# Memory's values as the last projection chunk, head weights in the retention steps, and one unit for a head's three branches in tiles 0 and 1

## The chip, the core and the metric

The kernel runs on one core of a Trainium2 chip. A core has TensorE for matmuls (PE; PEld are its weight loads), VectorE (DVE), ScalarE (ACT), GpSimd (POOL) and SyncE (SP, which here issues most loads). They run their own streams and meet at semaphores. The metric is the time of one execution on the device in microseconds, lower is better.

## What is computed

One step of a hybrid decoder layer, for a prompt of 1024 tokens and a sample group of 8 sequences with 8 tokens each. One input projection feeds three groups of heads, and the mixed result goes through an output projection and a final norm:

```python
def mixer_inputs(x, ln_g, w_in):
    B, T = x.shape[:2]
    h = rmsnorm(x, ln_g) @ w_in
    q_n, kv_c, kv_s, kv_w, g_n, z_n, q_r, k_r, v_r, z_r, q_m, z_m = split_cols(h)
...
    o_n = nsa_prompt(q_n, kv_c, kv_s, kv_w, g_n, comp)
    o_r, st_r = retention_prompt(q_r, k_r, v_r, pos_p, ret_gn[l])
    mkv = mem_kv(mem_prompt, ln_mem[l], w_mem_kv[l])
    o_m = mem_attend(q_m, mkv)
    xp = finish(xp, o_n, z_n, o_r, z_r, o_m, z_m, w_out[l])
...
    o_n, new_win = nsa_sample(q_n, kv_c, kv_s, kv_w, g_n, comp, cache_nsa_cmp[l], cache_nsa_slc[l],
                              cache_nsa_win[l], page_table)
```

The NSA heads (8 query heads in 2 groups) attend in three branches, each with its own softmax: selected blocks (slc), a window of 512 keys (win), and compressed blocks (cmp); sigmoid gates mix them. With 1024 keys in blocks of 64 and 16 blocks selected, the prompt's selected branch is plain causal attention. The retention heads end in a norm for each head, `(o - mu) * rsqrt(var + EPS)`, times weights `g`. The memory heads attend to 256 memory tokens, whose keys and values are a projection too. The new K and V rows, the shifted window cache (`new_win_s`, 4 MB copied from input to output) and the states are outputs.

## The kernel before, in words

All matmuls of the projections work on float32 numbers split into a high and a low part, three products for each. The program has three stages.

**Trunk.** The projection is cut into 15 column chunks (`CHUNKS`; an entry is source, first column, width; source 1 is the memory's weights), each of 256 columns or a few more, and 9 row tiles (8 of prompt, one of the sample's 64 tokens; the memory's chunks have 2 tiles). That makes 121 jobs, run chunk by chunk; a job is 24 matmuls of 0.119 us. The job's result stands in one of four PSUM banks until ACT (`ACT_CHUNKS`) or DVE evicts it, with a silu where it is a gate; POOL stores it to DRAM. Each chunk's weights are loaded by SP and split by ACT (high part) and DVE (low part, L568). Between jobs stand small groups of steps for compression and retention. Retention takes one step for each row tile: `scores`, `norm`, `state` on DVE. `finish` (L1295) makes the norm's factors for all nine tiles at once and applies, for each tile, the factor (L1305) and the head weights `gnb` (L1306). SP's `load_k` (L668) waits for `r_done`, which these last operations raise, then loads K's rows (`pk_Ktok`) over memory that the retention used. PE's `ktr` steps (L918) transpose them, between the last jobs.

**Attention.** A table of blocks sets the order. A block is a row tile `i` and a group `g`; blocks of two tiles alternate, tile pairs (6,1), (7,0), (5,2), (4,3). A block has four units (l = 4g to 4g + 3), for heads g and g + 4: two are the selected branch of one head, two are the window and compressed branches of one head. The block of g = 4 has two memory units. There are 144 units, numbered v. In iteration v the loop places: scores `qk` (L1703, L1706, L1707) and row maxima `max` (L2031, DVE) of unit v + 2; the transposes of the probabilities of unit v (L1733), up to four key tiles a chunk, copied from PSUM by ACT or DVE in turn (L1900); the value matmuls `pv` (L1853) of a pair of units; the exponentials `sm` (L1963, ACT) of unit v + 2; and from v = 8 one group of the sample's steps. A group is a few steps: transposes of cached keys from SBUF (L1785), scores (L1717), probabilities transposed (L1810), values (L1821). The sample's caches come in four page pairs: SP loads the window pages (`s_WG`, L1598) and 16 selected pages (`s_SG`, L1601) of each pair.

Some steps hang on the number v alone:

```python
            if v == 36:
                steps.append(("copy_win", 0))
            if v % 4 == 0 and 36 < v <= 60:
                steps.append(("copy_kv", (v - 36) // 4 - 1))
```

`copy_win` (L1986) is one DMA on ACT's queue that copies the window cache from DRAM to DRAM; `copy_kv` (L1991) are smaller ones of new K and V rows.

**Output projection.** PE multiplies the mixed rows by the output weights, DVE adds and normalizes.

## Time and profile before

| | |
|---|---|
| runs | 950.6, 950.07, 946.06 us; median 950.07 |
| profiled execution | 949.89 us, span of the core 948.1 us |
| PE, DVE, ACT, POOL busy | 910.6, 513.5, 413.9, 289.5 us |
| DMA | 118.10 MB, mean 125 GB/s |

How to read it: times in the rows are microseconds from the span's start. In a timeline row stand start, duration, engine, line, operation, output<-input, shapes and count; in brackets at the end is the idle time of the engine before the row, with the instruction or DMA that ended it. Matmuls overlap, so the duration of one is longer than the distance to the next. A trailing q (SPq, ACTq) marks the engine's issuing of a DMA. "DMA to landing" is the time from issue to the DMA's end. The granted clock is 1.00 at 2.4 GHz and 0.50 at 1.2 GHz. The trunk ends at about 484 us.

### The profile page before, as it was taken

Reading aid. Unit: us, or ns where it says so; the run is one execution under the profiler, and the core shown is the slowest. Engines: PE = TensorE matmul, PEld = TensorE weight load, DVE = VectorE, ACT = ScalarE, POOL = GpSimd, SP = SyncE. Lnnn points to the kernel's source line nnn. Section 1 sums busy time; section 2 is a strip of 40 time slices with the busy share of each in tenths; the row PEclk is TensorE's granted clock in tenths of the full one; section 3 lists DMA queues with packets and bytes.
Section 4 is the critical chain, followed back from the end, with each engine's and each line's share of the span. In section 5 each row is a group of like instructions: output and inputs, shape, how many; then the busy total and the mean of one; then the engine's idle time right before and its main releaser. Section 6 shows DMA issues by size and latency. Waiting matters only on the chain.

```text
span 948.1 us, 20735 instructions
## 1 busy us (share of the span) xinstructions
PE 910.6 (96%) x7830; PEld 828.3 (87%) x7830; DVE 513.5 (54%) x1304; ACT 413.9 (44%) x1061; POOL 289.5 (31%) x495
## 2 busy tenths in 40 slices
PE   6999999999999999999889999999999999999997
PEld 6999999999999999999888788878877787878885
DVE  5556332323223556347536687766776757845443
ACT  7443221234344111222446666656665667832221
POOL 0213222212216353453144253334322525410000
PEclk9999999999999999999999999999999999999999
DMA  8554422404242543321868059714504142334331
GB/s 227 174 188 141 142 81 111 160 29 120 71 148 76 137 134 105 103 87 53 201 172 212 3 158 263 251 55 140 156 1 130 56 138 65 114 122 140 125 127 66
DMA packets 85076, 118.10 MB, mean 125 GB/s; under 512 B 12914, under 2 KB 67234, under 8 KB 84402
## 3 DMA queue, kind: packets, MB, share of 16 engines
q1 hardware_dynamic: 71522, 73.30, 27.0%
q0 software_dynamic: 10224, 36.20, 11.6%
q10 hardware_dynamic: 3232, 7.28, 2.1%
q8 instruction: 63, 1.03, 0.5%
q14 instruction: 35, 0.29, 0.1%
HBM read 91.68 MB, written 32.02 MB: 130 GB/s over the span
## 4 chain that ended last, share of the span: by engine, by line
PE 77%; DVE 6%; issue 5%; DMA 4%; ACT 3%; POOL 2%; SPq 2%; ACTq 0%; DVEq 0%; POOLq 0%
PE psum L1853 7%; PE psum L592 7%; PE psum L593 6%; PE psum L594 6%; PE psum L1733 5%; PE psum L1706 4%; PE psum L1872 3%; PE psum L1873 3%; PE psum L1874 3%; PE psum L1707 3%; PE psum L579 2%; PE psum L580 2%; PE psum L581 2%; PE psum L834 2%; PE psum L836 2%
## 5 line engine op out<-in xcount | busy, mean ns | idle before, releaser
L592 PE MATMUL psum<-a_whi,f_xhi 128*128 128x256 f32 (+1 forms) x672 | 195.2, 290 | 2.5 <-DVE f_xlo L1053 1.4
L593 PE MATMUL psum<-a_wlo,f_xhi 128*128 128x256 f32 (+1 forms) x672 | 190.9, 284 | 0.0
L594 PE MATMUL psum<-a_whi,f_xlo 128*128 128x256 f32 (+1 forms) x672 | 190.2, 283 | 0.0
L1963 ACT ACTIVATE p_P<-psum,p_nb 128x640 f32<-128x640 f32 (+7 forms) x224 | 124.1, 560 | 40.0 <-DVE p_nb L2031 37.9
L2031 DVE TENSOR_REDUCE p_nb<-psum 128x1 f32<-128x640 f32 (+7 forms) x224 | 110.2, 522 | 48.8 <-PE psum L1707 45.2
L592 PEld LDWEIGHTS psum<-a_whi,f_xhi 128*128 128x128 f32 x672 | 127.8, 190 | 5.2 <-DVE a_wlo L568 1.8
L593 PEld LDWEIGHTS psum<-a_wlo,f_xhi 128*128 128x128 f32 x672 | 127.8, 190 | 0.0
L594 PEld LDWEIGHTS psum<-a_whi,f_xlo 128*128 128x128 f32 x672 | 127.7, 190 | 0.0
L736 POOL DMA_DIRECT2D h_scratch<-a_hst x93 | 51.1, 552 | 228.8 <-DVE a_hst L1114 105.6
L1733 PE MATMUL psum<-f_ident,p_P 128*128 128x128 f32 x656 | 99.7, 276 | 1.1 <-ACT s_KTw L1912 0.5
L1733 PEld LDWEIGHTS psum<-f_ident,p_P 128*128 128x128 f32 x656 | 77.7, 141 | 7.2 <-DVE p_PT L1900 1.7
L568 DVE SCALAR_TENSOR_TENSOR a_wlo<-a_wraw,c_gcol,a_whi 128x256 fp32r<-128x256 f32 (+1 forms) x120 | 55.4, 524 | 43.0 <-ACT a_whi L555 42.9
L1900 ACT COPY p_PT<-psum 128x512 f32<-128x512 f32 (+3 forms) x107 | 56.3, 526 | 47.6 <-PE psum L1733 46.6
L1123 DVE TENSOR_TENSOR c_ctlo<-psum,c_cthi 128x512 fp32r<-128x512 f32 (+1 forms) x40 | 25.4, 636 | 93.7 <-ACT c_cthi L1008 93.7
L1853 PE MATMUL psum<-p_PT,p_V 128*64 128x128 f32 x1056 | 71.8, 279 | 1.7 <-issue 1.3
L1008 ACT CAST c_cthi<-psum 128x512 fp32r<-128x512 f32 (+1 forms) x40 | 21.8, 544 | 106.3 <-PE psum L817 106.3
L1853 PEld LDWEIGHTS psum<-p_PT,p_V 128*64 128x64 f32 x1056 | 56.4, 136 | 12.4 <-issue 10.8
L2210 POOL TENSOR_TENSOR p_Oi<-p_Oi 128x128 f32<-128x128 f32 x32 | 16.6, 518 | 129.9 <-DVE p_Oi L2053 129.9
L579 PE MATMUL psum<-f_xhi,a_whi 128*128 128x256 f32 x192 | 55.6, 290 | 0.0
L1900 DVE COPY p_PT<-psum 128x512 f32<-128x512 f32 (+3 forms) x109 | 54.4, 499 | 1.2 <-PE psum L1733 1.2
L580 PE MATMUL psum<-f_xhi,a_wlo 128*128 128x256 f32 x192 | 54.1, 282 | 0.0
L581 PE MATMUL psum<-f_xlo,a_whi 128*128 128x256 f32 x192 | 53.8, 280 | 0.0
(334 smaller groups left out, 2139.2 us busy)
## 6 DMA issues: line engine op xcount, KB each, us to landing
a_wraw<-in_w_in SPq DMA_DIRECT2D x24, 512.0 KB, 4.4
h_scratch<-a_hst POOLq DMA_DIRECT2D x72, 128.0 KB, 3.5
s_SG<-in_cache_nsa_slc SPq DMA_DIRECT2D x64, 128.0 KB, 2.2
p_qd<-q_scratch SPq DMA_DIRECT2D x16, 384.0 KB, 7.7
a_xraw<-in_x_prompt SPq DMA_DIRECT2D x8, 512.0 KB, 6.8
s_MK<-in_cache_mem SPq DMA_DIRECT2D x8, 512.0 KB, 9.3
s_WG<-in_cache_nsa_win SPq DMA_DIRECT2D x8, 512.0 KB, 4.6
mix_scratch<-p_zt POOLq DMA_DIRECT2D x8, 512.0 KB, 3.4
```

The source lines that it names most:

```text
L568: ins = nc.vector.scalar_tensor_tensor(out=lo[:, k], in0=raw[:, k], scalar=split_gain(e, 4 * half + k), in1=hi[:, k].bitcast(F32), op0=ALU ...
L579: nc.tensor.matmul(out, wh, hi, start=first, stop=False)
L580: nc.tensor.matmul(out, wl, hi, start=False, stop=False)
L581: return nc.tensor.matmul(out, wh, lo, start=False, stop=last)
L592: nc.tensor.matmul(out, hi, wh, start=first, stop=False)
L593: nc.tensor.matmul(out, hi, wl, start=False, stop=False)
L594: return nc.tensor.matmul(out, lo, wh, start=False, stop=last)
L1733: l = nc.tensor.transpose(o[0:w, 128 * j:128 * j + 128], P[v % 2][:, at:at + w], ident[:])
L1853: i_mm = nc.tensor.matmul(psum[64 * j:64 * j + 64, at:at + 128], val, PTs[p_rank[pair[j]] % NPT][0:w, 128 * p:128 * p + 128], start=k == 0 ...
L1900: copy(PTs[r % NPT][0:w, 0:128 * n], bank(4 + c % 3)[0:w, 0:128 * n]).then_inc(sem, 1)
L1963: nc.scalar.activation(dst, s_view(s), ACT.Exp, bias=nb[:, g % NNB:g % NNB + 1], accum_out=ssum[:, par[i], s[1]:s[1] + 1]).then_inc(S("p_e ...
L2031: nc.vector.tensor_reduce(out=nb[:, g % NNB:g % NNB + 1], in_=s_view(s), op=ALU.max, axis=AX.X if len(s[6]) == 1 else AX.XY, negate=True). ...
```

## The change

1. The memory's value chunk moves from place 8 to the last place of the projection. ACT evicts it, with a scaled copy. The other chunks, their weights and splits come earlier by its two jobs. Its load for the attention (`VM`) moves from `load_k` to the start of the sample's loads and is waited for at the first memory unit.
2. The multiplication with `gnb` moves from `finish` into `norm` of each retention step, and `load_k` waits for those only. The last operations of `finish` follow later; `ktr` waits for the last state too.
3. ACT's load of the exponential's table, and DVE's low parts of the first Q tile (`qlo`), stand before the last two evictions of the trunk. Before, the table load was the attention's first step.
4. In tiles 0 and 1 (`WHOLE`) a unit (l >= 18) is all three branches of one head, so such a block has 2 units where it had 4, and there are 128 units. Two groups of the sample's steps are placed in such an iteration, except for the eight groups that begin with the first page pair's load. The copies out of `OT` (the values' transposes) are written before each new one. The numbers 36 and 40 to 60 in the code above stay.

```diff
--- before.py
+++ after.py
...
 CHUNKS = [(0, 512, 256), (0, 768, 256), (0, 1816, 256), (0, 2072, 256), (0, 2328, 256), (0, 1024, 280), (1, 0, 256), (0, 1304, 256),
-          (1, 256, 256), (0, 256, 256), (0, 2840, 256), (0, 0, 256), (0, 1560, 256), (0, 2584, 256), (0, 3096, 256)]
+          (0, 256, 256), (0, 2840, 256), (0, 0, 256), (0, 1560, 256), (0, 2584, 256), (0, 3096, 256), (1, 256, 256)]
 NCH = len(CHUNKS)
...
     BLOCKS = [(pair[j], g) for pair in PAIRS for j, g in ((0, 0), (0, 1), (1, 0), (1, 1), (0, 2), (1, 2), (1, 3), (1, 4), (0, 3), (0, 4))]
-    UNITS = [(i, l) for i, g in BLOCKS for l in (range(4 * g, 4 * g + 4) if g < 4 else (16, 17))]
+    WHOLE = (0, 1)
+    UNITS = [(i, l) for i, g in BLOCKS for l in ((16, 17) if g == 4 else (18 + 2 * g, 19 + 2 * g) if i in WHOLE else range(4 * g, 4 * g + 4))]
     NV = len(UNITS)
-    unit_block = [b for b, (i, g) in enumerate(BLOCKS) for _ in range(4 if g < 4 else 2)]
+    unit_block = [b for b, (i, g) in enumerate(BLOCKS) for _ in range(2 if g == 4 or i in WHOLE else 4)]
     last_of_block = {b: v for v, b in enumerate(unit_block)}
...
     assert all(prev[i] is None or of_tile[prev[i]][-1] < of_tile[i][0] for i in range(QT))
-    per_unit = lambda l: 1 if l < 16 and l % 4 < 2 else 2
+    per_unit = lambda l: 3 if l >= 18 else 1 if l < 16 and l % 4 < 2 else 2
     sm_before = [sum(per_unit(l) for _, l in UNITS[:v]) for v in range(NV)]
...
-    ACT_CHUNKS = (5, 7, 12, 13, 14)
-    MEM_CHUNKS = (6, 8)
-    Q_CHUNKS = (11, 9, 10)
+    ACT_CHUNKS = (5, 7, 11, 12, 13, 14)
+    MEM_CHUNKS = (6, 14)
+    Q_CHUNKS = (10, 8, 9)
...
                     steps.append(("load_w", fill.pop(0)[1]))
+        steps.extend([("table", 0), ("qlo", 0), ("qlo", 1), ("qlo", 2)])
         evict(0)
...
                 sp.wait_ge(S("r_stout"), 16 * 6)
-                wait_stored(sp, last_job[11])
+                wait_stored(sp, last_job[10])
                 for br, c in enumerate((C_KVS, C_KVW)):
...
                     sp.dma_start(V[:, br], hD[0:T, c + 128:c + 256].rearrange("(t p) n -> p t n", p=128)).then_inc(S("p_v"), 16)
-                sp.dma_start(VM[:], new_mem[:, 256:512].rearrange("(t p) n -> p t n", p=128)).then_inc(S("p_v"), 16)
...
                 pe.wait_ge(S(f"p_k{n // 2}"), 16)
+                pe.wait_ge(S("r_ns"), 4)
                 pe.wait_ge(S("r_done"), NT)
...
                 split_hi(act, n, (int(what == "split_b"),))
+            elif what == "table":
+                act.wait_ge(S("r_done"), 2 * NT)
+                nc.scalar.activation(small[:, 152:153], ident[:, 0:1], ACT.Exp).then_inc(S("p_table"), 1)
             elif what == "ev" and by_act(proj_jobs[n][0]):
...
                 act.wait_ge(S("x_rs"), NT + 2)
-                if j == 5:
+                if j == NCH - 1:
+                    nc.scalar.activation(dst[:, 0:256], src, ACT.Copy, scale=rstd(t)).then_inc(S("h_evac_act"), 1)
+                elif j == 5:
                     nc.scalar.activation(dst[:, 0:256], src[:, 0:256], ACT.Copy, scale=rstd(t)).then_inc(S("h_part"), 1)
...
                     nc.vector.tensor_tensor(lv, src, hv.bitcast(F32), ALU.subtract).then_inc(S("p_klo"), 1)
-            elif what == "qtr":
+            elif what == "qlo":
                 dve.wait_ge(S("q0_hi"), n + 1)
...
             ch.step(nc.vector.tensor_tensor(rsq[0:r], OC[0:r, n], OC[0:r, n], ALU.mult))
-            ch.step(nc.vector.tensor_reduce(out=var, in_=rsq[0:r].rearrange("p (h e) -> p h e", h=4), op=ALU.add, axis=AX.X))
+            ch.do(nc.vector.tensor_reduce(out=var, in_=rsq[0:r].rearrange("p (h e) -> p h e", h=4), op=ALU.add, axis=AX.X))
+            nc.vector.tensor_tensor(OC[0:r, n], OC[0:r, n], gnb[0:r], ALU.mult).then_inc(S("r_done"), 1)
+            ch.wait()
...
                 oc = OC[0:r, n].rearrange("p (h e) -> p h e", h=4)
-                ch.step(nc.vector.tensor_tensor(oc, oc, rs[0:r, 4 * n:4 * n + 4].rearrange("p (h o) -> p h o", o=1).to_broadcast([r, 4, HD]), ALU.mult))
-                nc.vector.tensor_tensor(OC[0:r, n], OC[0:r, n], gnb[0:r], ALU.mult).then_inc(S("r_done"), 1)
+                dve.wait_ge(S("r_done"), NT)
+                nc.vector.tensor_tensor(oc, oc, rs[0:r, 4 * n:4 * n + 4].rearrange("p (h o) -> p h o", o=1).to_broadcast([r, 4, HD]), ALU.mult).then_inc(S("r_done"), 1)
...
         base, at = 1024 * ((v + 1) % 2), sm_before[v]
+        if l >= 18:
+            g, j = (l - 18) // 2, l % 2
+            h, n = g + 4 * j, 128 * (i + 1)
+            return [(at, 6 * g + j, 0, h, 0, n, [(base, n)], 0), (at + 1, 6 * g + 2 + j, 1, h, 0, n, [(base + 512 + NC, n)], 256),
+                    (at + 2, 6 * g + 4 + j, 2, h, 0, 64, [(base + 512, NC)], 640)]
         if l >= 16:
...
         i, l = UNITS[v]
+        if l >= 18:
+            h, n = softmaxes(v)[0][3], softmaxes(v)[0][5]
+            base = softmaxes(v)[0][6][0][0]
+            return [(base, n, KS[:, h // 4, 0:n], h), (base + 512, NC + n, KW[:, h // 4, 0:NC + n], h)]
         if l < 16 and l % 4 >= 2:
...
             n = unit_block[v]
-            if v == last_of_block[n] and a == 1 and 128 * (k + 1) >= softmaxes(v)[a][5]:
+            if v == last_of_block[n] and a == len(softmaxes(v)) - 1 and 128 * (k + 1) >= softmaxes(v)[a][5]:
+                while outs:
+                    write(outs.pop(0)[0])
                 steps.append(("ot", n))
...
         groups = sample_groups()
+        n_groups = len(groups)
+        paged = next(k for k, g in enumerate(groups) if ("load_pair", 0) in g)
         first = 8
...
                 mine.append(add_p(v, tiles[f:f + 4]))
-                if l >= 16:
+                if l in (16, 17):
                     waiting.append((mine[-1], mine[-1]))
...
             partner = mine
-            while waiting and (l % 2 == 0 or l >= 16) and waiting[0][1] not in mine:
+            while waiting and (l % 2 == 0 or l == 17) and waiting[0][1] not in mine:
                 pv()
...
                     steps.append(("load_q", later[k]))
-            for what, n in groups.pop(0) if v >= first and groups else []:
-                if what == "t":
-                    add(n)
-                else:
-                    steps.append((what, n))
+            for _ in range(2 if l >= 18 and not 0 <= n_groups - len(groups) - paged < 8 else 1):
+                for what, n in groups.pop(0) if v >= first and groups else []:
+                    if what == "t":
+                        add(n)
+                    else:
+                        steps.append((what, n))
             if v == 36:
...
         load_mem(1)
+        sp.dma_start(VM[:], new_mem[:, 256:512].rearrange("(t p) n -> p t n", p=128)).then_inc(S("p_k2"), 16)
         for o, c, w in ((0, C_ZN, 512), (512, C_ZR, 256), (768, C_ZM, 256)):
...
+        first_mem = min(v for v in range(NV) if any(s[2] == 3 for s in softmaxes(v)))
+
         def pv(pair):
...
             if pair[0] == p_index[0]:
-                pe.wait_ge(S("p_v"), 48)
+                pe.wait_ge(S("p_v"), 32)
+            if v == first_mem:
+                pe.wait_ge(S("p_k2"), 32)
             wait_chunks_read(pe, pair)
-            if l >= 16:
+            if l in (16, 17):
                 sides = [[(p, k, 128) for p, (a, k, _) in enumerate(p_chunks[pair[0]][2]) if a == j] for j in range(2)]
...
                     p, k, w = sides[j][m]
-                    vj = v if l >= 16 else v + j
-                    a = j if l >= 16 else p_chunks[pair[j]][2][p][0]
+                    vj = v if l in (16, 17) else v + j
+                    a = j if l in (16, 17) else p_chunks[pair[j]][2][p][0]
                     _, num, b, h, k0, keys = softmaxes(vj)[a][0:6]
...
     def act_attend(act):
-        nc.scalar.activation(small[:, 152:153], ident[:, 0:1], ACT.Exp).then_inc(S("p_table"), 1)
         act.wait_ge(S("h_mm"), len(proj_jobs))
...
```

DVE at the end of the trunk. Before, the tail of the norm, with `f_OC` the retention outputs and `r_gnb` the head weights:

```order
L1298 TENSOR_SCALAR f_small<-f_small 128x36
L1300 RECIPROCAL f_small<-f_small 128x36
L1310 TENSOR_TENSOR f_small<-f_small 128x36
L1311 TENSOR_TENSOR f_small<-f_small 128x36
L1312 TENSOR_SCALAR f_small<-f_small 128x36
L1313 TENSOR_TENSOR f_small<-f_small 128x36
L1305 TENSOR_TENSOR f_OC<-f_OC,f_small 128x256
L1306 TENSOR_TENSOR f_OC<-f_OC,r_gnb 128x256
```

After, in the same place, behind the last state (`r_kvt`, `r_BDs`):

```order
L1298 TENSOR_TENSOR r_kvt<-r_kvt,r_BDs 128x512
L1300 TENSOR_SCALAR r_BDs<-r_kvt,f_colc 128x2x128 x2
L1307 TENSOR_SCALAR f_small<-f_small 128x36
L1309 RECIPROCAL f_small<-f_small 128x36
L1319 TENSOR_TENSOR f_small<-f_small 128x36
L1320 TENSOR_TENSOR f_small<-f_small 128x36
L1321 TENSOR_SCALAR f_small<-f_small 128x36
L1322 TENSOR_TENSOR f_small<-f_small 128x36
L1315 TENSOR_TENSOR f_OC<-f_OC,f_small 128x256 x8
L1315 TENSOR_TENSOR f_OC<-f_OC,f_small 64x256
```

The multiplications with `r_gnb` have left the tail; one stands in each retention step.

ACT where trunk and attention meet. `a_hst` are evicted rows, `p_P` the probabilities of the first units. Before:

```order
L996 ACTIVATE a_hst_70<-psum,f_small 128x256
L996 ACTIVATE a_hst_71<-psum,f_small 128x256
L996 ACTIVATE a_hst_68<-a_hst_68,f_small 64x256
L1940 ACT_TABLE_LOAD
L1940 ACTIVATE f_small<-f_ident 128x1
L1963 ACTIVATE p_P_119,p_ssum<-psum,p_nb 128x896
L1963 ACTIVATE p_P_120,p_ssum<-psum,p_nb 128x896
```

After:

```order
L1003 ACTIVATE a_hst_69<-psum,f_small 128x256
L1003 ACTIVATE a_hst_70<-a_hst_70,f_small 64x256
L985 ACT_TABLE_LOAD
L985 ACTIVATE f_small<-f_ident 128x1
L998 ACTIVATE a_hst_71<-psum,f_small 128x256
L998 ACTIVATE a_hst_68<-psum,f_small 128x256
L1990 ACTIVATE p_P_119,p_ssum<-psum,p_nb 128x896
L1990 ACTIVATE p_P_120,p_ssum<-psum,p_nb 128x896
```

The table load has moved ahead of the last two evictions, and these are now the memory's values.

ACT around the copy of the window cache. Before, `s_KTs` are the sample's transposed selected keys, and 128x1024, 128x640 the exponentials of tile 7's first units:

```order
L1963 ACTIVATE p_P_119,p_ssum<-psum,p_nb 128x640
L1963 ACTIVATE p_P_119,p_ssum<-psum,p_nb 128x64
L1912 COPY s_KTs<-psum 128x512
L1986 DMA out_new_win_s<-in_cache_nsa_win 8x8x16128
L1900 COPY p_PT_147<-psum 128x512
L1963 ACTIVATE p_P_120,p_ssum<-psum,p_nb 128x640
L1963 ACTIVATE p_P_120,p_ssum<-psum,p_nb 128x64
L1946 ACTIVATE s_PW,s_ssm<-s_PW,s_snb 128x576
L1900 COPY p_PT_129<-psum 128x512
L1963 ACTIVATE p_P_119,p_ssum<-psum,p_nb 128x1024
```

After, 128x128 and 128x64 are those of tile 0's whole units and 128x1088 the sample's selected keys of a sequence pair:

```order
L1990 ACTIVATE p_P_119,p_ssum<-psum,p_nb 128x128 x2
L1990 ACTIVATE p_P_119,p_ssum<-psum,p_nb 128x64
L1973 ACTIVATE s_PSl,s_ssm<-s_PSl,s_snb 128x1088
L2013 DMA out_new_win_s<-in_cache_nsa_win 8x8x16128
L1928 COPY p_PT_145<-psum 128x384
L1990 ACTIVATE p_P_120,p_ssum<-psum,p_nb 128x128 x2
L1990 ACTIVATE p_P_120,p_ssum<-psum,p_nb 128x64
L1946 COPY s_PTS<-psum 128x512
L2011 COPY p_OT<-psum 128x384
L1990 ACTIVATE p_P_119,p_ssum<-psum,p_nb 128x1024
```

The copy's issue has moved from the first unit of block (7,0) to the first of block (0,0), behind an exponential of the sample.

## Rows read from the trace of the kernel before

**Rows 1.** Page, busy time: engine, us, share of the span, instructions.

```profile
PE 910.6 (96%) x7830; PEld 828.3 (87%) x7830; DVE 513.5 (54%) x1304; ACT 413.9 (44%) x1061; POOL 289.5 (31%) x495
```

**Rows 2.** Waits of PE, whole span: line, releaser; us in total, times, longest.

```profile
PE psum L1703 <- ACT p_P L1963: 4.2, 6, 1.4
```

**Rows 3.** Timeline 442 to 461 us: start, us, engine, line, op, out<-in, count [idle before].

```profile
442.68 3.26 DVE L568 SCALAR_TENSOR_TENSOR a_wlo<-a_wraw,c_gcol,a_whi 128x256 fp32r<-128x256 f32 x8
...
447.66 0.42 DVE L1305 TENSOR_TENSOR f_OC<-f_OC,f_small 128x256 f32<-128x256 f32 x1
...
454.47 0.42 DVE L1306 TENSOR_TENSOR f_OC<-f_OC,r_gnb 64x256 f32<-64x256 f32 x1
...
454.91 1.01 SPq L668 DMA_DIRECT2D pk_Ktok<-h_scratch  x2
...
460.25 1.41 PE L918 MATMUL psum<-f_ident,pk_Ktok 128*128 128x128 f32 x8 [3.71 <-DMA pk_Ktok<-h_scratch]
```

**Rows 4.** Lines L661 and L668: ns min/median/max, first and last start; time to landing.

```profile
L661 SPq DMA_DIRECT2D out_new_ret_s<-r_BDs x4: 596/642/649, 442.7 to 444.7; - x4
...
DMA to landing us min/median/max: 2.6/2.7/2.7
...
L668 SPq DMA_DIRECT2D pk_Ktok<-h_scratch x2: 386/482/577, 454.9 to 455.3; - x2
...
DMA to landing us min/median/max: 5.3/6.0/6.7
```

**Rows 5.** Windows: stretch, length, busy us of each engine, PE clock, DMA share, GB/s.

```profile
460.30:464.20 3.90, 3.90 (x21) 3.90 (x22) 2.55 (x4) 2.79 (x5) 0.60 (x3) 0.57 1.14 286
488.00:492.00 4.00, 3.94 (x22) 3.88 (x23) 1.42 (x3) 2.05 (x5) 4.00 (x8) 0.57 0.66 174
...
597.90:604.00 6.10, 6.10 (x89) 5.64 (x87) 2.74 (x9) 3.25 (x16) 4.20 (x8) 1.00 1.05 322
```

**Rows 6.** Timeline 485 to 489 us, ACT and then PE.

```profile
485.00 0.51 ACT L996 ACTIVATE a_hst<-a_hst,f_small 64x256 f32<-64x256 f32 x1 [3.25 <-DVE a_hst L1099]
485.52 1.28 ACT L1940 ACT_TABLE_LOAD   x1
486.82 0.20 ACT L1940 ACTIVATE f_small<-f_ident 128x1 f32<-128x1 f32 x1
...
485.56 0.23 PE L1703 MATMUL psum<-p_maskb,f_identb 128*128 128x128 bf16 x1 [1.51 <-ACT a_hst L996]
...
488.06 0.37 PE L1703 MATMUL psum<-p_maskb,f_identb 128*128 128x128 bf16 x3 [1.40 <-ACT p_P L1963]
```

**Rows 7.** Timeline 584 to 587 us, PE.

```profile
584.59 1.31 PE L1853 MATMUL psum<-p_PT,p_V 128*64 128x128 f32 x20
585.73 0.39 PE L1853 MATMUL psum<-p_PT,f_VC 128*64 128x128 f32 x4
586.05 0.66 PE L1785 MATMUL psum<-f_ident,s_SG 128*128 128x128 f32 x4
```

**Rows 8.** Timeline, ACT's DMA issues of units 36 and 44.

```profile
573.89 0.83 ACTq L1986 DMA_DIRECT2D out_new_win_s<-in_cache_nsa_win  x1
...
596.02 0.51 ACTq L1991 DMA_DIRECT2D out_new_slc_p<-h_scratch  x1
```

**Rows 9.** DMA queues, 575.5 to 597.9 us: queue; packets, MB, share of 16 engines.

```profile
q10 hardware_dynamic: 640, 4.58, 52.9%
```

**Rows 10.** Tile p_qd, 577 to 579 us: issues, and time to landing.

```profile
L692 SPq DMA_DIRECT2D p_qd<-q_scratch x2: 573/614/655, 577.1 to 577.7; - x2
...
DMA to landing us min/median/max: 7.3/17.9/28.4
```

**Rows 11.** Timeline 606 to 626 us, SP and then PE.

```profile
606.27 17.27 SPq L1601 DMA_DIRECT2D s_SG<-in_cache_nsa_slc  x16
...
618.60 0.60 PE L1785 MATMUL psum<-f_ident,s_WG 128*128 128x128 f32 x4
...
625.51 0.63 PE L1785 MATMUL psum<-f_ident,s_SG 128*128 128x128 f32 x4 [0.47 <-DMA s_SG<-in_cache_nsa_slc]
```


## The prediction, made before the change was timed

> **What bounds the kernel now.** I read the engines' busy time first: PE works 910.6 of 948.1 us [rows 1], so a change pays only where it takes idle time, low clock or work from PE, and it costs where it makes PE wait. The waits of PE by cause come next: six on the exponentials before score matmuls sum to 4.2 us [rows 2], and three waits at the end of the trunk, each seen beside its row in the timeline, are among the largest of all. Then I followed those backwards: who released PE, and what held that one.
>
> The sum is made against the profiled execution, 949.89 us. The median of the three runs is 950.07, so no correction is needed between them.
>
> **Part 1: the head weights and memory's last chunk.** At the end of the trunk DVE splits a weight chunk in eight operations from 442.68 us (3.26 us), then runs the GroupNorm's tail: from 447.66 us nine pairs of dependent operations, the last one starting at 454.47 [rows 3]. SP has waited for that and issues the load of K's rows at 454.91; the first of its two loads lands 5.3 us later [rows 3, 4]. PE has finished its matmuls at 456.5, stands for 3.71 us and starts the K transposes at 460.25 [rows 3].
> The change moves nine multiplications by the head weights into the retention steps (0.42 us each, beside matmuls, where DVE is busy 54% of the time [rows 1]) and takes the K load out from behind the tail. What releases the load then is the last state store. Those four stores were issued over 2.0 us from 442.7 and each takes 2.7 us to land [rows 4]. In the new order half of a weight split (some 1.6 of the 3.26 us) stands ahead of the last state, so the stores end at about 442.7 + 1.6 + 2.1 + 2.7 = 449.1, and the first K load lands at 449.1 + 5.3 = 454.4, ahead of PE's 456.5. PE's new wait there, for the states, ends well before it arrives; behind it stand the K transposes and all the rest of PE. The wait goes. So does what follows it: from 460.3 to 464.2 the granted clock is 0.57 [rows 5], that is between 1.2 GHz (0.50) and 2.4 GHz, after 3.71 us without work. Low clock costs 3.90 x (1 - 0.57) = 1.7 us. **Part 1: -5.4 us**, between -6.0 and 0 (zero if the load is still late by another path; the memory K load behind it has the same slack).
> Moving the memory value chunk to the end reorders the same 121 jobs. Every job finds its weights split two jobs sooner or later; the matmuls are the same in number. The memory values are loaded after the sample's cache reads, and are first used by a pair of memory units tens of us later: nothing.
>
> **Part 2: the switch from trunk to attention.** After the last projection matmuls PE waits 1.51 us at 485.56 for ACT's silu of the last sample job (485.00, 0.51 us, after two DVE additions), and 1.40 us at 488.06 for the exponential of unit 0, which stands behind the 1.28 us load of the exponential's table at 485.52 and a first tiny activation at 486.82 [rows 6]. Afterwards, 488 to 492, the clock is 0.57 [rows 5]: 4.0 x 0.43 = 1.7 us. In all 1.51 + 1.40 + 1.7 = 4.6 us. The last chunk's silu is now a plain scaled copy without the DVE additions, and the table load stands two evictions earlier, hidden by matmuls. ACT waits there for the GroupNorm's tail, with two evictions queued behind it; the tail, now nine operations, is over by some 453 us, nearly 30 us sooner. What is late next is the maximum of unit 1 and its exponential: 0.3 to 0.7 us remain before the third unit's scores, and part of the low clock. I take **-3.4 us**, between -4.6 (nothing left) and -1.3 (only the table hidden).
> Of the table: the load takes 1.28 us and the next activation starts 1.30 us after it, so hiding it is worth 1.3 us by the row. The Trainium skill (ScalarE: Activation LUTs, What ACT_TABLE_LOAD costs) gives 1283 ns for the load, which the trace agrees with, plus about 1380 ns of drain, which no gap in these rows shows; by the page the switch would be worth 2.66 us, and the sum some 1.3 us lower.
>
> **Part 3: three branches in one unit, tiles 0 and 1.** 32 units of two kinds become 16; the matmuls are the same. PE gains where sequences merge: four value matmuls at 585.73 take until 586.05, 0.32 us, while twenty before them took 1.14 us, 0.057 each [rows 7], so the end of a group costs 0.32 - 0.23 = 0.09 us, and its start about as much by the same way of reading: 0.2 us a group. Eight groups fewer give 1.5 us. ACT's and DVE's copies of transposed probabilities become fewer and larger. Idle PE time in these tiles' blocks is short, part of the 4.2 us of [rows 2]. But a longer chain (three maxima, then three exponentials) stands between a unit's scores and its transposes, with two sample groups popped per unit, so that dependent sample steps come closer to each other. I take **-2.3 us**, between -5 (all idle gone too) and +5 (each of eight joints exposed by 0.6 us, a little under the 0.7 us, 4.2/6, that a wait of rows 2 lasts at the mean).
>
> **Part 4: what the renumbering moves.** The copy of the window cache (4 MB, issued by ACT) hangs on unit number 36. Before, unit 36 is the first of block (7,0) and the copy is issued at 573.89; another copy, of unit 44, the first of block (0,0), is issued at 596.02 [rows 8]. After, tile 1's blocks have 8 units fewer, so unit 36 is the first of (0,0): **the big copy is issued where 596 to 598.6 is now**, about 24 us later. What does it do while it runs? From 575.5 to 597.9 its queue takes 52.9% of the time of all 16 DMA engines [rows 9]. Of the two loads of the next tile's Q issued at 577.1 and 577.7 one needs 7.3 us to land and the other 28.4 [rows 10]. So a load beside the copy in effect lands only after it ends: its packets alternate with far larger ones.
> Before, that stretch lies between the loads of the sample's first page pair and those of the second, whose 16 page loads are issued from 606.27 on, over 17.27 us; PE turns the window pages from 618.60 and the first selected page at 625.51, where it waits 0.47 us for the DMA already [rows 11]. After, the second pair's loads start some ten us behind the copy's issue and beside it. The copy starts 1.6 us after its issue and runs 22.4, so it ends between 620 and 622.6; I take the later, as it stands behind an exponential in its unit. Then 3 MB are waiting (1 MB window, 2 MB selected pages), half of them on the engines that the copy held. At the 322 GB/s of 597.9 to 604 [rows 5] that takes 9.8 us, at the pace of the K load (1 MB in 7.1 us from 454.91, less 2 us of start: 5 us a MB [rows 4]) 15 us. Window pages would be there at 626 to 628. PE has more prompt work before their second transposes in the new order, my estimate is 4.2 us, so that in the old frame it wants them at 618.6 + 4.2 = 622.8: 3.2 to 5.3 us of wait. The selected pages follow until 632.4 to 637.6, against a want of 625.9 plus that wait: 3 to 6 us more, so 8 to 11.5 us together, and low clock after each long wait as in parts 1 and 2, 1.7 us or a little more. **+12.3 us**, from 0 (the loads get through) to +17.
> The Trainium skill (DMA: Bandwidth & Descriptors, Queues, rings and completion order) states that each DMA engine goes round robin between its queues packet by packet. By that rule a queue of small packets beside one of large packets gets few bytes; with rows 9 and 10 the trace agrees.
>
> **Sum.** 949.89 - 5.4 - 3.4 - 2.3 + 12.3 = 951.1; forecast **951 us**, within 0.5%. A measurement here tells about 0.5% from no change: 4.75 us, 945.3 to 954.8.
>
> **Rivals.**
> *The page loads get through* (chance 0.29). For: half of the first Q load's bytes moved early, the copy holds only half of the engines, and pages are small. Against: 28.4 us in rows 10. Then parts 1 to 3 stand alone: 949.9 - 11.1 = 938.8; with a collision of a third of the size 943.
> *The collision is large and the whole units cost* (0.20). Mechanism: at the second page pair PE waits for pages at 15 us for 3 MB, and because two sample groups are popped per unit it meets page after page with nothing between; with part 3 at +2: 949.9 - 5.4 - 3.4 + 2 + 14 = 957. It decides from a collision above 13 us, or part 3 above +2 with 12.
> *The trunk's end doesn't do what it says* (0.05). K's load could stay late, since the transposes now wait for the states as well. Without part 1, and with the collision: 956.5. For: the state stores are a chain of their own. Against: 2.1 us of slack worked out above.
> *As forecast, gains cancelled* (0.46), own range 945.5 to 954.5.
>
> **How the numbers follow.** Faster by over 0.5%: 0.29. Within: 0.46. Slower: 0.20 + 0.05 = 0.25. The range takes in the first rival from its clean value of 938.8 and the second to 958.
>
> **What would show it.** Part 1: no idle PE before the K transposes and clock 1.00 behind them. Part 2: table load before the last two evictions, PE waits of under 1 us before the second and third unit's scores. Part 3: fewer and larger copies, 1 to 2 us less PE time in tiles 1 and 0. Part 4: the large copy issued at about 585 to 590 us of the new span (11 earlier by parts 1 to 3), Q and page loads landing in over 10 us, PE waits with page transposes as the waiting line, 5 us or more, and a clock of 0.5 to 0.6 behind them. The forecast is wrong if those page transposes don't wait, or if a wait comes up in the first tiles that no row of before shows.

## The result: slower by 1.2%

| | runs | median us | ratio to before (95%) |
|---|---|---|---|
| before | 4 | 948.58 | |
| after | 4 | 960.21 (959.09 to 961.93) | 1.0121 (1.0103 to 1.0139) |

The profiled execution of after has a span of 960.1 us, against 948.1. The forecast was 951, the range ended at 958: wrong, and on the side of slower.

### The profile page after: what moved, and what is told of

It is laid out like the page before. It is cut to its first block, busy times and chain, and to the rows that moved or that the text cites. A ratio compares the mean times of both kernels' runs of the same rounds, so it can differ in the third digit from the quotient of the medians.

```text
span 960.1 us, 20679 instructions
## 1 busy us (share of the span) xinstructions
PE 915.8 (95%) x7830; PEld 831.3 (87%) x7830; DVE 516.9 (54%) x1298; ACT 414.4 (43%) x1059; POOL 289.0 (30%) x495
## 3 DMA queue, kind: packets, MB, share of 16 engines
q8 instruction: 63, 1.03, 0.4%
## 4 chain that ended last, share of the span: by engine, by line
PE 78%; DVE 6%; issue 5%; ACT 4%; DMA 2%; SPq 2%; POOL 2%; ACTq 0%; DVEq 0%; POOLq 0%
PE psum L1881 8%; PE psum L594 7%; PE psum L595 7%; PE psum L596 7%; PE psum L1757 5%; PE psum L1730 3%; PE psum L1900 3%; PE psum L1901 3%; PE psum L1902 3%; PE psum L1731 3%; PE psum L835 2%; ACT p_P L1990 2%; PE psum L837 2%; PE psum L836 2%; PE psum L581 2%
## 5 line engine op out<-in xcount | busy, mean ns | idle before, releaser
L2058 DVE TENSOR_REDUCE p_nb<-psum 128x1 f32<-128x640 f32 (+8 forms) x224 | 109.3, 523 | 54.3 <-PE psum L1731 47.4
L1990 ACT ACTIVATE p_P<-psum,p_nb 128x640 f32<-128x640 f32 (+8 forms) x224 | 123.8, 561 | 29.8 <-DVE p_nb L2058 27.3
L1757 PE MATMUL psum<-f_ident,p_P 128*128 128x128 f32 x656 | 97.6, 276 | 4.0 <-ACT s_PTS L1946 1.7
L570 DVE SCALAR_TENSOR_TENSOR a_wlo<-a_wraw,c_gcol,a_whi 128x256 fp32r<-128x256 f32 (+1 forms) x120 | 63.7, 592 | 27.0 <-ACT a_whi L557 26.8
L2237 POOL TENSOR_TENSOR p_Oi<-p_Oi 128x128 f32<-128x128 f32 x32 | 14.5, 454 | 154.0 <-DVE p_Oi L2080 154.0
L1928 DVE COPY p_PT<-psum 128x512 f32<-128x512 f32 (+3 forms) x104 | 52.0, 500 | 1.3 <-PE psum L1757 1.1
```

The lines of the kernel that those rows point to most:

```text
L570: ins = nc.vector.scalar_tensor_tensor(out=lo[:, k], in0=raw[:, k], scalar=split_gain(e, 4 * half + k), in1=hi[:, k].bitcast(F32), op0=ALU ...
L1757: l = nc.tensor.transpose(o[0:w, 128 * j:128 * j + 128], P[v % 2][:, at:at + w], ident[:])
L1928: copy(PTs[r % NPT][0:w, 0:128 * n], bank(4 + c % 3)[0:w, 0:128 * n]).then_inc(sem, 1)
L1990: nc.scalar.activation(dst, s_view(s), ACT.Exp, bias=nb[:, g % NNB:g % NNB + 1], accum_out=ssum[:, par[i], s[1]:s[1] + 1]).then_inc(S("p_e ...
L2058: nc.vector.tensor_reduce(out=nb[:, g % NNB:g % NNB + 1], in_=s_view(s), op=ALU.max, axis=AX.X if len(s[6]) == 1 else AX.XY, negate=True). ...
```

## The profile after

PE's busy time, in the page's row of the engines, answers to [rows 1]:

```profile
PE 915.8 (95%) x7830; PEld 831.3 (87%) x7830; DVE 516.9 (54%) x1298; ACT 414.4 (43%) x1059; POOL 289.0 (30%) x495
```

5.2 us more busy, for the same 7830 matmuls, and the mean granted clock of the core fell from 0.995 to 0.985. The other part is waiting. PE's waits in the whole span, the largest that are new, against [rows 2] (in a row: who waited, for what; us in total, times, longest; "issue" means that the profile shows no one that PE waited for):

```profile
PE psum L1809 <- DMA s_SG<-in_cache_nsa_slc: 3.6, 1, 3.6
PE psum L1741 <- ACT s_KTs L1940: 2.9, 2, 2.4
PE psum L1809 <- DMA s_WG<-in_cache_nsa_win: 2.5, 1, 2.5
...
PE psum L1842 <- issue: 2.3, 2, 1.8
PE psum L581 <- DVE a_hst L1119: 2.0, 2, 1.8
```

Four of the five lie in the sample's steps: pages (`s_SG`, `s_WG`), the copy of their transposes (`s_KTs`), and value matmuls (L1842). The last, for DVE's eviction of a projection job (`a_hst`), stands in the trunk.

The end of the trunk, DVE, SP and PE, in the timeline, answers to [rows 3]:

```profile
450.16 3.10 DVE L1315 TENSOR_TENSOR f_OC<-f_OC,f_small 128x256 f32<-128x256 f32 x9
...
453.22 1.00 SPq L670 DMA_DIRECT2D pk_Ktok<-h_scratch  x2
...
460.46 1.04 PE L920 MATMUL psum<-f_ident,pk_Ktok 128*128 128x128 f32 x8
```

The tail of the norm is six and more products without a wait between them (2.10 us for six); the K load is issued at 453.22, and PE's transposes start at 460.46 with no idle time ahead of them. The missing wait came as forecast, though the issue is four us later than the forecast's 449.1; PE gets there four us later too. The switch to attention, which answers to [rows 6], came in part: waits of 0.57 and 1.18 us where 1.51 and 1.40 stood (both were to be under 1), and the clock behind them is 1.00 instead of 0.57 (the last row is a window, with the columns of [rows 5]).

```profile
483.22 0.23 PE L1727 MATMUL psum<-p_maskb,f_identb 128*128 128x128 bf16 x1 [0.57 <-ACT a_hst L998]
...
485.49 0.32 PE L1727 MATMUL psum<-p_maskb,f_identb 128*128 128x128 bf16 x3 [1.18 <-ACT p_P L1990]
...
485.00:490.00 5.00, 4.51 (x38) 4.40 (x39) 3.28 (x7) 4.37 (x11) 4.27 (x9) 1.00 0.59 153
```

Then the second page pair. In the timeline, ACT's issue of the big copy, SP's issues of window and selected pages, and PE's transposes and scores of them; this answers to [rows 8] and [rows 11]:

```profile
592.96 0.84 ACTq L2013 DMA_DIRECT2D out_new_win_s<-in_cache_nsa_win  x1
...
604.79 0.96 SPq L1621 DMA_DIRECT2D s_WG<-in_cache_nsa_win  x2
606.54 22.21 SPq L1624 DMA_DIRECT2D s_SG<-in_cache_nsa_slc  x16
...
621.97 1.94 PE L1809 MATMUL psum<-f_ident,s_WG 128*128 128x128 f32 x8 [2.52 <-DMA s_WG<-in_cache_nsa_win]
...
631.35 1.09 PE L1809 MATMUL psum<-f_ident,s_SG 128*128 128x128 f32 x4 [3.55 <-DMA s_SG<-in_cache_nsa_slc]
...
638.74 1.98 PE L1741 MATMUL psum<-s_KTs,s_QP 128*64 128x512 f32 x4 [2.43 <-ACT s_KTs L1940]
```

The copy goes out at 592.96, almost twelve us ahead of the window pages. The sixteen page issues take 22.21 us instead of 17.27. PE waits 2.52, 3.55 and 2.43 us. The times to landing of the window pages and of the sixteen selected ones, one line each, median in the middle:

```profile
DMA to landing us min/median/max: 5.9/11.2/16.6
...
DMA to landing us min/median/max: 2.2/4.3/11.2
```

A window load needs up to 16.6 us, a page up to 11.2; before it was 6.9 and 4.5 in the same places. The clock through the waits, with the columns of [rows 5]:

```profile
620.00:624.00 4.00, 2.03 (x12) 2.00 (x12) 0.81 (x3) 1.03 (x7) 0.00 (x0) 0.70 0.86 263
624.00:628.00 4.00, 3.80 (x15) 1.77 (x12) 1.50 (x6) 1.79 (x8) 0.00 (x0) 0.50 0.85 256
628.00:632.00 4.00, 0.65 (x3) 0.68 (x4) 0.91 (x2) 0.42 (x1) 0.00 (x0) 0.50 0.68 225
632.00:636.00 4.00, 4.00 (x28) 3.36 (x27) 1.31 (x4) 0.62 (x2) 0.00 (x0) 0.59 0.01 4
```

PE runs at 0.50 to 0.70 for sixteen us. So the loads are late beside the copy, where it was forecast. The question for the runs was how large it is, and what else costs.

## The experiments

Twelve kernels ran, each beside the kernel before, whose median was 949.2 us with e1 to e4, 948.93 with e5 to e8 and 948.85 with e9 to e12. The last column is the ratio's distance from 1, times 949 us. Differences of the medians give up to 1.2 us more or less (2.9 for e10), so a tenth of a us means nothing here.

| run | median us | ratio (95%) | that is, of 949 us |
|---|---|---|---|
| e1: after, copies where they were | 954.42 | 1.0050 (1.0030 to 1.0070) | +4.7 |
| e2: before, copies moved | 962.58 | 1.0143 (1.0094 to 1.0192) | +13.6 |
| e3: after, no whole units | 944.96 | 0.9963 (0.9942 to 0.9984) | -3.5 |
| e4: after, copy in small pieces | 959.25 | 1.0110 (1.0064 to 1.0156) | +10.4 |
| e5: e3, split of chunk 9 earlier | 943.19 | 0.9948 (0.9931 to 0.9964) | -4.9 |
| e6: before, head weights alone | 945.00 | 0.9963 (0.9949 to 0.9977) | -3.5 |
| e7: whole units in tile 1 alone | 948.94 | 1.0007 (0.9991 to 1.0024) | +0.7 |
| e8: e1, one group a unit in tile 0 | 948.45 | 0.9997 (0.9977 to 1.0018) | -0.3 |
| e9: e2, copy in small pieces | 954.58 | 1.0054 (1.0036 to 1.0072) | +5.1 |
| e10: before, small copies moved | 951.76 | 1.0018 (0.9999 to 1.0036) | +1.7 |
| e11: e1, the two groups apart | 947.07 | 0.9975 (0.9962 to 0.9989) | -2.4 |
| e12: tile 1, groups apart, split earlier | 945.51 | 0.9956 (0.9937 to 0.9975) | -4.2 |

### Copies back in their place (e1)

```diff
-            if v == 36:
+            if v == 28:
                 steps.append(("copy_win", 0))
-            if v % 4 == 0 and 36 < v <= 60:
-                steps.append(("copy_kv", (v - 36) // 4 - 1))
+            if v in (32, 36, 38, 40, 44, 46):
+                steps.append(("copy_kv", (32, 36, 38, 40, 44, 46).index(v)))
```

> The changed kernel, with the big window-cache copy and the six small copies back at the blocks where the kernel before has them: the big one at unit 28, the first of block (7,0), the small ones at units 32, 36, 38, 40, 44, 46. Nothing else differs. Theory A (the copy beside the second page pair's loads costs the time): the waits of PE on window and selected pages vanish, the stretch from block (7,2) to (7,3) gets back 14 to 17 us, and the time is 943 to 947 us. Theory B (the whole units and the doubled sample groups cost it, the copy is only there): the time stays within 3 us of the changed kernel's 960, and the waits move to scores and probabilities in tile 0's blocks.

954.4 us: neither. 1.0121 - 1.0050 is 6.7 us given back by the copies (the two intervals allow 4 to 9), but 8.3 us remain against e3, which has no whole units. PE's waits:

```profile
PE psum L1809 <- DMA s_SG<-in_cache_nsa_slc: 2.9, 1, 2.9
PE psum L1741 <- ACT s_KTs L1940: 2.5, 2, 2.0
PE psum L1842 <- issue: 2.3, 2, 1.8
```

The wait for the window pages is gone. The wait for a selected page (2.9), for the copy of transposes (2.5) and at L1842 (2.3) are still there, with no copy of the window cache beside them. The pages themselves land in 2.0 to 3.7 us, as before; PE asks for them sooner. So a second cause exists, and these waits lie in and beside tile 0's blocks. What the wait for `s_KTs` is made of, in order of time, ACT and PE:

```profile
630.96 1.06 PE L1809 MATMUL psum<-f_ident,s_SG 128*128 128x128 f32 x4
...
632.54 0.78 ACT L1973 ACTIVATE s_PW<-s_PW,s_snb 128x576 f32<-128x576 f32 x1
...
633.30 0.59 ACT L1940 COPY s_KTs<-psum 128x512 f32<-128x512 f32 x1
...
634.03 1.08 PE L1741 MATMUL psum<-s_KTs,s_QP 128*64 128x512 f32 x4 [2.01 <-ACT s_KTs L1940]
```

PE has transposed pages and stands until ACT has copied the result. ACT takes the copy in its turn, behind two exponentials of a memory unit and one of the sample (L1973). The 1.8 us at L1842 are of the same kind: there the copy of the transposed probabilities, 601.16 to 601.75, stands behind an exponential of 128x1024, and PE starts at 601.85.

### The copies alone, moved in the kernel before (e2, e10)

e2 is the kernel before with

```diff
-            if v == 36:
+            if v == 44:
                 steps.append(("copy_win", 0))
-            if v % 4 == 0 and 36 < v <= 60:
-                steps.append(("copy_kv", (v - 36) // 4 - 1))
+            if v in (52, 56, 64, 68, 72, 76):
+                steps.append(("copy_kv", (52, 56, 64, 68, 72, 76).index(v)))
```

and e10 has the second half of it only (the big copy stays at unit 36).

> The kernel before, with only the copies moved: the big one from unit 36 to unit 44, the first of block (0,0), the small ones from units 40 to 60 to units 52, 56, 64, 68, 72, 76, which are the blocks where the changed kernel has them. Theory A: 10 to 15 us slower than before, 959 to 964 us, with PE waiting for window and selected pages and a low clock behind each wait. Theory B: no difference, within 2 us of 949.

> The kernel before with the big copy at its place (unit 36) and only the six small copies moved to units 52 to 76. If the small copies take their part in the 13.4 us, 951 to 955 us, with PE waiting for selected pages; if the big copy alone does it, 948 to 950 us.

e2: 13.6 us slower (8.9 to 18.2). PE's two waits, in the timeline; then the window loads' and the sixteen page issues' rows (the duration of an issue in ns, min/median/max, and the window loads' time to landing):

```profile
624.01 1.09 PE L1785 MATMUL psum<-f_ident,s_WG 128*128 128x128 f32 x4 [6.41 <-DMA s_WG<-in_cache_nsa_win]
...
635.73 1.09 PE L1785 MATMUL psum<-f_ident,s_SG 128*128 128x128 f32 x4 [3.09 <-DMA s_SG<-in_cache_nsa_slc]
...
DMA to landing us min/median/max: 6.0/12.9/19.7
...
L1601 SPq DMA_DIRECT2D s_SG<-in_cache_nsa_slc x16: 337/338/9114, 605.4 to 631.1; - x16
```

6.41 and 3.09 us of waiting, with low clock behind each (0.50 over 624 to 628 us, 0.66 over 635 to 640). A window load took up to 19.7 us. One page issue kept SP for 9114 ns instead of 338, and SP handed out no load in that time. e10 shows the part of the small copies, 1.7 us (an interval that just touches none): their issues lie beside the page loads, and PE waits 3.21 us for a page instead of 0.47.

```profile
626.40 0.63 PE L1785 MATMUL psum<-f_ident,s_SG 128*128 128x128 f32 x4 [3.21 <-DMA s_SG<-in_cache_nsa_slc]
...
619.92 0.51 ACTq L1991 DMA_DIRECT2D out_new_slc_p<-h_scratch  x1
```

### Pieces of 4 KB instead of 64 KB (e4, e9)

```diff
-                act.dma_start(io["new_win_s"][0, :, 0:WIN - DS].rearrange("b t a k d -> b (t a k d)").rearrange("b (c e) -> b c e", c=16),
...
+                for d in range(2):
+                    act.dma_start(io["new_win_s"][0, :, 0:WIN - DS].rearrange("b t a k d -> b (t a k d)").rearrange("b (c f e) -> b f c e", c=63, f=2)[:, d],
...
```

> The changed kernel, copy at unit 36 as it is, but cut into pieces of 4 KB instead of 64 KB: two DMAs of 8 x 63 pieces, every second piece each, the same bytes. Theory A1 (the loads are starved because engines alternate between queues piece by piece, and the copy's pieces are large): page loads land in 3 to 6 us beside the copy, PE's waits for pages shrink below 2 us together, the time is 944 to 949 us. Theory A2 (the copy takes bytes, whatever their pieces): the page loads still land after the copy ends and the time stays at 957 to 962 us.

> The kernel before with the copies moved as in the run with the big copy at unit 44 (962.6 us), and the big copy cut into pieces of 4 KB. If the pieces' size starves the page loads, most of the 13.4 us come back: 950 to 954 us. If the bytes do, or the small copies that follow, 959 to 963 us.

On the kernel before (e9) it gives back 8.4 of the 13.6 us (3.5 to 13.4 by the two intervals); one wait for the sample's loads is left:

```profile
621.17 1.09 PE L1785 MATMUL psum<-f_ident,s_WG 128*128 128x128 f32 x4 [3.93 <-DMA s_WG<-in_cache_nsa_win]
...
DMA to landing us min/median/max: 6.3/11.8/17.2
```

The window load's worst time falls only from 19.7 to 17.2 us, but the wait for a selected page is gone. On the changed kernel (e4) almost nothing comes back: 1.0 us, within an interval of 4.7 us to either side. There the wait moved, from the window pages to a selected page:

```profile
PE psum L1809 <- DMA s_SG<-in_cache_nsa_slc: 7.2, 1, 7.2
...
DMA to landing us min/median/max: 3.7/5.6/9.9
```

The median page load takes 5.6 us there against 4.3 in after. So piece size matters on the kernel before, and it isn't all there: the copy's bytes and the small copies stay beside the loads, and no run parts the two. Why the same edit is worth 8.4 us on one kernel and 1 on the other was not settled; the changed kernel asks for its pages sooner, which is the next finding.

### No whole units (e3), and in tile 1 alone (e7)

```diff
-    WHOLE = (0, 1)
+    WHOLE = ()
```

> The changed kernel with no tile in WHOLE: four units a block everywhere, 144 units, so the copies stand where they stand before; memory's values last, head weights in the retention steps, table load early remain. Both theories of the collision: none here. By the block starts of the two traces the trunk's parts are worth 2.2 us at the first maximum and 4.2 us four units later: 944.5 to 947 us. If moving the copy (the run with the copy at unit 28) and this one give the same time, whole units are worth nothing.

> The changed kernel with whole units in tile 1 alone (tile 0 has four units a block again), the copies at the blocks of the kernel before (the big one at unit 28, the first of block (7,0)). By the block starts of the two traces whole units in tile 1 gain 0.8 us and in tile 0 with its doubled sample groups lose 8. Theory C (tile 0 loses): 943.5 to 946 us. If whole units lose in both tiles, 949 or more.

e3 came as expected: the trunk's parts are worth 3.5 us together. e7 didn't: it is 4.2 us slower than e3, so whole units with two groups in tile 1 lose too. Two of PE's waits, at block (2,2), where e3 has one of 0.24 us:

```profile
701.94 0.66 PE L1757 MATMUL psum<-f_ident,p_P 128*128 128x128 f32 x4 [1.03 <-ACT p_PT L1928]
...
703.50 0.44 PE L1757 MATMUL psum<-f_ident,p_P 128*128 128x128 f32 x2 [0.57 <-ACT s_PTS L1946]
```

The sample's steps have moved against the blocks. These two waits can hardly be what makes e7 slow, though: e11 and e12 below have them as well (1.03 and 0.58 us in e12), at 947.07 and 945.51 us. e7's runs spread from 947.3 to 953.4 us, the longer ones at a lower mean clock (0.994 against 0.999), and the profiled one is among the shortest. Where the 4.2 us lie stays open.

### Two groups together (e8, e11)

Both have the copies where e1 has them. e8 places one sample group in an iteration of tile 0 (`l >= 18 and i == 1` for two), and two in each of the later iterations 92 to 95. e11 keeps two and sets them apart:

```diff
             partner = mine
+            if l >= 18 and not 0 <= n_groups - len(groups) - paged < 8:
+                place_group()
             while waiting and (l % 2 == 0 or l == 17) and waiting[0][1] not in mine:
...
-            for _ in range(2 if l >= 18 and not 0 <= n_groups - len(groups) - paged < 8 else 1):
...
+            place_group()
```

> The changed kernel with whole units in both tiles and the copies at the blocks of the kernel before, but one sample group an iteration in tile 0 instead of two; four later iterations (92 to 95) take two so that all groups find a place. Theory C (the selected pages come one in 1.08 us, and the doubled groups ask for them sooner): the 2.9 us wait for a page and the 2.0 us wait for its copy go, 944 to 948 us. Theory D (the whole units' own chain of three maxima and exponentials costs it): the loss in tile 0's blocks stays, 951 to 955 us.

> The changed kernel with the copies at the blocks of the kernel before (as in the run with the copy at unit 28), and the two sample groups of a whole unit's iteration apart: one right behind the transposes of the unit, before its value matmuls, the other at the iteration's end as before. The pace of the groups and the whole units stay. Theory C2 (two groups standing together are the cost: the second one asks for pages a unit sooner, and meets copies that the first has just asked for): 945 to 950 us against 954.4. Theory D (whole units' own chains): 953 to 956 us.

e11 gives back 7.1 of the 8.3 us with whole units and all their softmaxes unchanged. PE's waits in it, the largest behind the one for `in_ln_mem`:

```profile
PE psum L1813 <- DMA s_SG<-in_cache_nsa_slc: 2.8, 1, 2.8
PE psum L1731 <- ACT p_P L1994: 2.1, 4, 1.2
```

The page wait stands (2.8), but the wait of 2.0 us for `s_KTs` and that of 1.8 us at L1842 are gone from the list (L1846 here). Low clock is part of the loss too. The stretch 620 to 650 us in e1, e11 and e3, with the columns of [rows 5]:

```profile
620.00:650.00 30.00, 24.94 (x168) 19.24 (x166) 17.31 (x37) 14.64 (x42) 7.36 (x13) 0.83 0.11 31
...
620.00:650.00 30.00, 27.57 (x231) 22.41 (x233) 19.57 (x40) 16.78 (x45) 12.85 (x19) 0.89 0.21 51
...
620.00:650.00 30.00, 28.16 (x270) 23.02 (x271) 21.50 (x49) 20.05 (x59) 14.01 (x22) 1.00 0.20 48
```

That is 5.1, 3.3 and 0 us of low clock. All of PE's waits from 484 to 945 us sum to 21.3, 15.7 and 14.0 us in the three traces. From e1 to e11 that makes 5.6 us of waiting and 1.8 of clock, near the measured 7.1. In e8, where the second group of each unit comes later by a unit or more, the page wait goes too, and with it the low clock (1.00 over 620 to 650):

```profile
PE psum L1727 <- ACT p_P L1990: 3.2, 7, 1.2
```

So the units' own chain of three maxima and exponentials is at most a small part of the cost: e11 is 1.1 us over e3. Two groups side by side are most of it. What a step leaves to ACT is wanted by the next step at once, while the copy stands behind ACT's exponentials; with value matmuls between the groups PE has work in that time. The page wait has another reason, the pace of two groups a unit: the pages are wanted sooner, from loads that SP issues one by one in 17.3 us. e11 keeps that pace and the wait, e8 loses both. e8 is still 3.2 us over e3, and its runs spread from 944.9 to 952.4 us; that rest was not taken apart.

### The trunk: head weights alone (e6), and a split beside GpSimd (e5)

e6 is the kernel before with only the edits in `norm` and `finish` and the wait for `r_ns`. e5 is e3 with the split of weight chunk 9 moved:

```diff
-                if j + 1 < NCH and i == (0 if j in MEM_CHUNKS else 4):
+                if j + 1 < NCH and i == (0 if j in MEM_CHUNKS else 1 if j == 8 else 4):
...
-                if j + 1 < NCH and i == (1 if j in MEM_CHUNKS else 5):
+                if j + 1 < NCH and i == (1 if j in MEM_CHUNKS else 2 if j == 8 else 5):
```

> The kernel before, with one part of the change alone: the multiplication by the head weights in each retention step, K's load released by those, the last state waited for before the K transposes. Chunk order, table load and units as before. Predicted share of the trunk: the 2.4 to 3.7 us wait before the K transposes is gone and the low clock behind it, where there was one: 944 to 946.5 us. If the gain of the trunk came from the table load and the last chunk instead, 948 to 949.

> The changed kernel with no whole units, and with the split of weight chunk 9 three jobs earlier, at jobs 1 and 2 of chunk 8 instead of 4 and 5, so that it runs on DVE before GpSimd's first two rope steps. Theory R (the split is slow because GpSimd's tensor operations run beside it: one operation took 3.19 and 3.42 us instead of 0.47): no split operation over 1.2 us there, the 1.8 us wait of PE near 306 us is gone, 942 to 943.5 us against 945 without the move. Theory S (the split is slow for its own sake or its data): the long operations move with it, and the time stays at 945 within 1 us.

e6 alone gives the 3.5 us that the three edits of the trunk give together in e3. That points to a cost in the others that eats their gain. One shows in the timeline of after, at the first retention steps, DVE, then POOL, then PE, and last the line's own row:

```profile
297.44 8.29 DVE L570 SCALAR_TENSOR_TENSOR a_wlo<-a_wraw,c_gcol,a_whi 128x256 fp32r<-128x256 f32 x4
...
297.51 2.81 POOL L783 TENSOR_TENSOR r_rtmp<-r_rr,r_rt 128x256 f32<-128x256 f32 x4
...
302.65 2.78 POOL L783 TENSOR_TENSOR r_rtmp<-r_rr,r_rt 128x256 f32<-128x256 f32 x4
...
306.12 0.38 PE L581 MATMUL psum<-f_xhi,a_whi 128*128 128x256 f32 x1 [1.83 <-DVE a_hst L1119]
...
L570 DVE SCALAR_TENSOR_TENSOR a_wlo<-a_wraw,c_gcol,a_whi x120: 466/481/3425, 7.4 to 470.4; 128x256 fp32r<-128x256 f32 x112, 128x280 fp32r<-128x280 f32 x8
```

Four split operations take 8.29 us on DVE; of the 120 in the trace the median is 481 ns, and the largest 3425 (the last row, ns min/median/max). GpSimd runs its rope steps at that time, and DVE's eviction, behind the split, keeps PE 1.83 us. In e5 the same eight operations stand before the rope:

```profile
287.86 1.68 DVE L570 SCALAR_TENSOR_TENSOR a_wlo<-a_wraw,c_gcol,a_whi 128x256 fp32r<-128x256 f32 x4 [6.41 <-ACT a_whi L557]
...
291.58 1.65 DVE L570 SCALAR_TENSOR_TENSOR a_wlo<-a_wraw,c_gcol,a_whi 128x256 fp32r<-128x256 f32 x4
...
297.42 2.82 POOL L783 TENSOR_TENSOR r_rtmp<-r_rr,r_rt 128x256 f32<-128x256 f32 x4
```

1.68 and 1.65 us, the wait near 306 is gone, and the time is 943.19 us. The step from e3 to e5 is 1.4 us by the ratios, whose intervals overlap, so the gain in time is likely and not shown; that the split is slow beside its neighbour the rows show, in both orders. The Trainium skill (SBUF — State Buffer, SBUF: two separate sides) says that VectorE operations with two SBUF inputs and GpSimd operations that read SBUF take a shared pair of ports as an exclusive lock for a whole instruction. The split reads two SBUF tensors. Two of its operations took 3.19 and 3.42 us, each over four GpSimd products of some 0.7 us (2.81 and 2.78 us together), and the two between them 0.95. That VectorE is held up while GpSimd works agrees with the page; that it is held over four instructions in a row is more than one instruction's lock, and no run here explains it.

### A candidate (e12)

> A candidate: the changed kernel with whole units in tile 1 alone, their two groups apart, the copies at the blocks of the kernel before, and the split of weight chunk 9 three jobs earlier. Sum of what the runs gave: 943.2 us without whole units; if groups apart make whole units worth the 1.5 us of fewer value groups less what they expose, 941.5 to 943.5 us; if whole units shift the sample's steps as in the run with tile 1 alone (949 against 945), 946 to 947 us.

945.51 us, between its two cases, and not better than e5. Against e7 it has the groups apart and the split moved. It is 4.8 us faster by the ratios, but only 1.2 by the spans of the two traces (944.6 and 945.8), and the traces have the same large waits in the attention; what the groups apart are worth in tile 1 stays open. **e5 beats both kernels**: 943.19 us, 0.9948 of before (0.9931 to 0.9964) and 17 us under the changed kernel by the medians. It has the trunk's edits, the split moved, and no whole unit.

## Why the prediction was wrong

**Part 1, forecast -5.4, measured -3.5 us (e6, -2.2 to -4.8).** The mechanism was right: no idle time ahead of the K transposes. The size was off: I took the wait of 3.71 us and the 1.7 us of low clock behind it from one execution, as if they were always there. The traces of e2, e9 and e10 have the same trunk; their wait is 2.4, 2.5 and 2.3 us, and the clock behind it 1.00.

**"Every job finds its weights split two jobs sooner or later"**, put at nothing, is the step that failed in the trunk. The splits moved two jobs against GpSimd's rope, and the one of chunk 9 fell under it: 1.8 us of waiting, in every profile that has this order without the split moved, and in after's and e8's low clock besides (0.91 over 300 to 320 us). I had looked at what the splits wait for, not at what runs beside them.

**Part 2, forecast -3.4.** The idle time fell by 1.51 + 1.40 - 0.57 - 1.18 = 1.16 us and the clock behind it stayed at 1.00, which [rows 5] priced at 1.7: 2.9 us in this profile. That clock was no accident of one execution: it is 0.50 to 0.72 behind the switch in all five traces that have the old one, and 1.00 in all nine that have the new one. By the times, e5 against e6, the chunk order, the table and the last eviction together are worth 1.4 us, and the intervals allow anything from nothing to 3.5. So 3.4 was rather high, and isn't excluded.

**Part 3, forecast -2.3, measured +8.3 (e1 against e3).** This term had the wrong sign, and it is what lost the forecast. I had named the mechanism (dependent sample steps come closer), but bounded it at +5 by the mean wait of [rows 2] and took -2.3. Those rows are of a program whose groups stand a unit apart; they say nothing of two that stand together, and nothing of ACT's copies behind its exponentials (2.0 and 1.8 us of waiting) or of low clock behind the waits (5.1 us). [rows 11] had the hint: PE waited 0.47 us for a page already, so there was no slack to ask for one sooner. The 1.5 us gained by fewer value groups no run measures alone. An estimate from the traces: e11's span is 3.1 us longer than e3's, its waits 1.7 and its low clock 3.3 us more, which leaves some 1.9 us of work saved.

**Part 4, forecast +12.3, measured +6.7 in the changed kernel (after against e1), +13.6 on the kernel before (e2).** The place was right; the issue came at 592.96, three us behind the forecast's 585 to 590. The mechanism was right too, loads that land after up to 16.6 us and PE waiting for them. The size was about twice too large for the kernel that it was made for. Its sum took the page wait as the copy's alone, while 2.9 us of waiting for a page come from part 3 without any copy (e1); that would make the two terms overlap, but no run parts them. Two numbers in it stand in no row: the 4.2 us of more prompt work, and the 625.9 at which the page was to be wanted.

**Sum.** before, e3, e1 and after differ by one step at a time (the trunk's edits, whole units, the copies' place), so the steps add up by themselves: -3.5 (trunk) + 8.3 (whole units) + 6.7 (copies) = +11.5, the measured 1.0121. Against the forecast the trunk is 5.3 us worse, whole units 10.6 worse and the copies 5.6 better. Trunk and copies cancel by luck, and the miss is as large as that of part 3 alone. The nearest rival was "the collision is large and the whole units cost", at 957 and a chance of 0.20. Its price took +2 for part 3, where 8.3 was measured.

## To carry to other kernels

When units are merged or renumbered, look for everything that hangs on the number: a copy that stood between two bursts of loads cost 13.6 us beside one in e2, and 6.7 us in the changed kernel. Steps that stand together after a merge need a price of their own, from rows where such steps are neighbours, or from the slack of what they wait for, the queue of the engine between them included. When an order changes, compare what now runs at the same time on VectorE and GpSimd, not only who waits for whom.

## What the runs showed of the hardware

Two VectorE operations with two SBUF inputs took 3.19 and 3.42 us instead of 0.48 while four GpSimd products each ran beside them. SP's issue of one 128 KB load took 9.1 us instead of 0.34 in e2 and 5.3 us in after, where a 4 MB copy had been issued eight and twelve us before the window loads. Cutting that copy's pieces from 64 KB to 4 KB, with the same bytes, gave back 8.4 of 13.6 us on one kernel and 1 on another. Low clock behind the wait for K came in one execution of the same trunk, with a wait of 3.7 us, and not in three others, with 2.3 to 2.5. Over 460 to 480 us of before and of e2 (wait 2.4) the clock was 0.91 and 1.00:

```profile
460.00:480.00 20.00, 19.75 (x155) 19.75 (x156) 9.39 (x14) 10.45 (x20) 4.69 (x9) 0.91 0.99 224
...
460.00:480.00 20.00, 19.83 (x169) 19.62 (x167) 9.40 (x14) 10.94 (x21) 4.69 (x9) 1.00 1.02 241
```
